# Two transformer blocks on one core: a ninth ring slot, held weight chunks spread, the last scatter ahead of modulation, and the last norm on token rows

## What is computed

```python
mod = silu(c) @ w_ada[i] + b_ada[i]            # 6 x 1024 for the tokens, as many for ctx
h = modulate(rmsnorm(x, g_norm1[i]), sh1, sc1)
ka, va, kb, vb, qa, qb, u, v, gates = _split(h @ w_in[i], KV_SIZES + Q_SIZES)
x = x + gt1 * branch_merge(ya, yb, yc, gates, w_branch[i], w_out[i])
h2 = modulate(rmsnorm(x, g_norm2[i]), sh2, sc2)
x = x + gt2 * ec_moe(h2, w_router[i], w_e1[i], w_e3[i], w_e2[i])
```

## Time and profile before

| | |
|---|---|
| median of 3 runs | 2883.66 us (2879.49 to 2886.35) |
| the profiled execution | 2883.96 us, its span 2882.2 us |
| TensorE busy | 2611.2 us, 91% |
| VectorE, ScalarE, GpSimd busy | 810.2, 449.5, 55.4 us |
| moved by the DMA engines | 663.81 MB, mean 230 GB/s |
| mean granted TensorE clock | 0.957 of full speed |

### The profile page before, as it was taken

How to read it: one execution, slowest core, us unless ns; L and a number is a source line. 1 busy time by engine, 2 the same in 40 slices (tenths; PEclk the granted TensorE clock), 3 DMA queues, 4 the chain that set the end, 5 groups by cost and what they waited for, 6 DMA issues and landing times.

```text
span 2882.2 us, 30967 instructions
## 1 busy us (share of the span) xinstructions
PE 2611.2 (91%) x13335; PEld 1547.2 (54%) x13335; DVE 810.2 (28%) x1764; ACT 449.5 (16%) x1002; POOL 55.4 (2%) x85
## 2 busy tenths in 40 slices
PE   8999999999999999999999898987999998666665
PEld 5678878578873445444444342332556885232322
DVE  2535511435512454332121121112344422010101
ACT  1320010230011022222021101112111311000001
POOL 1000000000003000000000000000200000000000
PEclk9999999999999999999999999999999999776877
DMA  8654444464456111121527999999721367999996
GB/s 276 222 162 149 173 161 146 163 217 146 169 173 168 67 59 59 44 73 59 204 105 324 420 421 421 421 421 386 178 88 67 124 262 322 421 421 421 420 421 259
DMA packets 201019, 663.81 MB, mean 230 GB/s; under 512 B 13426, under 2 KB 58784, under 8 KB 151732
## 3 DMA queue, kind: packets, MB, share of 16 engines
q1 hardware_dynamic: 192912, 641.97, 58.2%
q0 software_dynamic: 7776, 19.81, 3.1%
q10 hardware_dynamic: 196, 0.06, 0.0%
HBM read 660.67 MB, written 9.57 MB: 233 GB/s over the span
## 4 chain that ended last, share of the span: by engine, by line
PE 72%; DMA 23%; DVE 3%; ACT 2%; issue 1%; ACTq 0%; DVEq 0%
PE ps L506 40%; DMA ring<-in_w_e 22%; PE ps L527 8%; PE ps L1120 7%; PE ps L687 5%; PE ps L1074 1%; PE ps L622 1%; PE ps L1100 1%; PE ps L935 1%; PE ps L957 1%; PE ps L890 1%; PE ps L903 1%; DMA ring<-in_w_ada 1%; PE ps L878 1%; PE ps L553 1%
## 5 line engine op out<-in xcount | busy, mean ns | idle before, releaser
L506 PE MATMUL ps<-normed,ring 128*128 128x256 f32 (+1 forms) x3456 | 942.8, 433 | 12.4 <-ACT normed L2012 8.8
L506 PEld LDWEIGHTS ps<-normed,ring 128*128 128x128 f32 x3456 | 653.6, 191 | 279.3 <-issue 201.3
L1120 PE MATMUL ps<-ring,arena 128*32 128x256 f32 (+1 forms) x4384 | 595.4, 527 | 195.6 <-DMA ring<-in_w_e 187.3
L1120 PEld LDWEIGHTS ps<-ring,arena 128*32 128x32 f32 (+1 forms) x4384 | 194.9, 133 | 576.7 <-DMA ring<-in_w_e 286.8
L506 PE MATMUL ps<-arena,ring 128*128 128x256 f32 (+1 forms) x832 | 254.0, 462 | 1.3 <-DVE small L1248 1.3
L527 PE MATMUL ps<-ring,normed 128*128 128x512 f32 x512 | 222.8, 593 | 0.0
L506 PEld LDWEIGHTS ps<-arena,ring 128*128 128x128 f32 x832 | 156.1, 190 | 88.1 <-issue 73.1
L1329 DVE COPY arena<-ps 128x256 f32<-128x256 f32 (+1 forms) x102 | 55.9, 554 | 418.4 <-PE ps L506 173.1
L527 PEld LDWEIGHTS ps<-ring,normed 128*128 128x128 f32 x512 | 96.2, 190 | 116.2 <-issue 116.1
L687 PE MATMUL ps<-arena,ring 128*128 128x256 f32 x704 | 152.3, 379 | 0.0
L687 PEld LDWEIGHTS ps<-arena,ring 128*128 128x128 f32 x704 | 133.8, 190 | 18.2
(11 more groups left out here) (252 smaller groups left out, 1788.9 us busy)
## 6 DMA issues: line engine op xcount, KB each, us to landing
ring<-in_w_e SPq DMA_DIRECT2D x366, 1024.0 KB, 17.8
ring<-in_w_in SPq DMA_DIRECT2D x56, 1024.0 KB, 7.4
ring<-in_w_ada SPq DMA_DIRECT2D x48, 1024.0 KB, 7.4
ring<-in_ffn_w_up SPq DMA_DIRECT2D x88, 512.0 KB, 5.9
ring<-in_ffn_w_down SPq DMA_DIRECT2D x22, 1024.0 KB, 5.0
ring<-in_dil_w_qkv SPq DMA_DIRECT2D x18, 1024.0 KB, 5.1
arena<-in_w_e SPq DMA_DIRECT2D x14, 1024.0 KB, 13.2
ring<-in_sb_w_qkv SPq DMA_DIRECT2D x12, 1024.0 KB, 12.9
```

The lines of the kernel that those rows point to most:

```text
L506: ins = mm(o[:, 0:n], slots[k // 4][:, k % 4, f * P:(f + 1) * P], src[:, k, 0:n], start=k == 0, stop=k == kts - 1)
L1120: ins = mm(o[w * g:w * g + w, 0:cols], lhs(2 * c + j), slot[:, j, g * cols:(g + 1) * cols], start=c == 0 and j == 0, stop=c == KT // 2 - 1 ...
```

## The change

1. `NSLOT` = 9. Room for it comes from the constants (the tables of stick-breaking, 896 words, now go to the arena and are loaded when the rows staged there are used up; one unused table is dropped) and from a smaller scratch for DMA descriptors (4096 for 8192 bytes).
2. The chunks set aside are given by place, `ASIDE_AT`: in layer 0 numbers 8, 13, 18, 22, 27, 31, 36 and 40 of the experts' list, in layer 1 numbers 8 to 17.
3. Router: two parts (layer 0; one in layer 1) stand before the first transposes, one fold (none) and the last part behind them, and the last two folds behind the second transposes.
4. The two panels between the last expert of layer 0 and `scatter(3)` go: these two panels are now the ones used behind layer 1's sum of squares, with both folds before the first panel of `w_in`, and the last two panels follow that first panel.
5. The last norm: TensorE transposes X itself, ScalarE squares the token rows out of PSUM with a sum for each row, and VectorE multiplies the same PSUM rows by the row's factor and the gain (a row broadcast to all partitions, loaded at expert 12 of layer 1). The store is issued by token tiles, two times 512 KiB.
6. POOL: the dilated bias goes in three pieces each way, both layers' neighbourhood biases are written sheared during the first block, each to a tensor of its own, and the position tiles wait until VectorE has emptied the second panel of `w_in` (`tile_turn`).

```diff
-NSLOT = 8
+NSLOT = 9
+ASIDE_AT = ((8, 27, 22, 40, 18, 36, 13, 31), (8, 9, 10, 11, 12, 13, 14, 15, 16, 17))
...
         for c0 in (6, 7, 0, 1, 4, 2, 3, 5):
             panel(w, c0 * BRANCH)
+            if i and c0 == 6:
+                ada_panels(ADA_LAYER // 2)
...
-        held = [len(out) + NSLOT + j for j in range(ASIDE_FIRST[i] + ASIDE_THEN)]
+        held = [len(out) + at for at in ASIDE_AT[i]]
...
         if i == 0:
-            ada_panels(ADA_LAYER)
+            ada_panels(ADA_LAYER // 2)
...
             pe.wait_ge(loads["consts"], 16)
+            pe.wait_ge(loads["sb_tables"], 16)
...
                 if last:
                     ada_part()
                     ada_part()
+                    ada_fold()
+                    ada_fold()
                 gemm_T(1, H, qtok, fresh=True)
+                if last:
+                    ada_part()
+                    ada_part()
+                gemm_N(1, H, qtiles)
                 if last:
                     ada_fold()
                     ada_fold()
-                gemm_N(1, H, qtiles)
...
+                for _ in range(ADA_ROUTER[i] - 1):
+                    ada_part()
                 pe.wait_ge(aff_ready.sem, aff_ready.nth("pe"))
...
-                ada_gap(ADA_ROUTER[i])
+                for _ in range(ADA_ROUTER[i] - 2):
+                    ada_fold()
+                ada_part()
                 pe.wait_ge(pos_ready.sem, pos_ready.nth("pe"))
...
+                ada_fold()
+                ada_fold()
                 pe.wait_ge(P_ready.sem, P_ready.nth("pe"))
...
-                if not last:
-                    ada_part()
-                    ada_part()
                 scatter(3)
-                if not last:
-                    ada_fold()
-                    ada_fold()
...
-            mean_square(H, S)
-            for _ in range(KT // GRP):
-                pe.wait_ge(h_ready.sem, h_ready.nth("pe"))
-            for t in range(ST):
-                for half in range(2):
-                    o = banks.open("a")
-                    if banks.due:
-                        pe.wait_ge(*banks.due)
+            for half in range(2):
+                pe.wait_ge(banks.freed["v"], scattered[4 * half - KT + 3])
+                for t in range(ST):
+                    o = banks.open("a", "v")
+                    pe.wait_ge(*banks.due)
                     for f in range(4):
-                        ins = nc.tensor.transpose(o[:, f * P:(f + 1) * P], H[:, 4 * half + f, t * P:(t + 1) * P], ident)
+                        ins = nc.tensor.transpose(o[:, f * P:(f + 1) * P], X[:, 4 * half + f, t * P:(t + 1) * P], ident)
...
-            sp.wait_ge(final_ready.sem, final_ready.nth("sp"))
-            sp.dma_start(out[0].rearrange("(t p) d -> p t d", p=P), OUTT).then_inc(loads["out"], 16)
+            for t in range(ST):
+                sp.wait_ge(final_ready.sem, 2 * t + 2)
+                sp.dma_start(out[0, t * P:(t + 1) * P, :], OUTT[:, t, :]).then_inc(loads["out"], 16)
...
-            pre_norm(X, g_final)
+            v.wait_ge(ssq_ready.sem, ssq_ready.nth("v"))
+            ve.tensor_tensor(RCOL[:, 0:ST], SSQ[:, 0:ST, 0], SSQ[:, 0:ST, 1], ALU.add).then_inc(total_ready.sem, total_ready.up())
...
+            for t in range(ST):
+                for half in range(2):
+                    d = slice(half * 512, (half + 1) * 512)
+                    ve.scalar_tensor_tensor(OUTT[:, t, d], turned[t, half], RCOL[:, t:t + 1], FINAL_GAIN[:, d], ALU.mult, ALU.mult
+                                            ).then_inc(final_ready.sem, final_ready.up())
...
                 norm(X, 2 * S)
+                if last:
+                    ada_copies(ADA_LAYER // 2)
                 scale_shift(i, 0, 2)
...
-            norm(X, S)
+            table(LOG_EXP)
+            for half in range(2):
+                for t in range(ST):
...
+                    ins = se.activation(OUTT[:, t, half * 512:(half + 1) * 512], o, ACT.Square, accum_out=SSQ[:, t, half:half + 1])
...
+            for i in range(DEPTH):
+                gp.dma_start(rpb_scratch[:, :, 48:48 + 2 * NA_WIN_C - 1], a["na_rpb_2"][i]).then_inc(loads["rpb_out"], 16)
...
+                gp.wait_ge(tile_turn.sem, tile_turn.nth("gp"))
                 for hh in range(2):
...
+            gp.wait_ge(dma_free.sem, dma_free.nth("gp"))
+            gp.dma_start(FINAL_GAIN, dram(a["g_final_2"], 0, [[0, P], [1, D]])).then_inc(loads["final_gain"], 16)
...
-    nc = bacc.Bacc("TRN2", target_bir_lowering=False, num_devices=1, dynamic_dma_scratch_size=8192)
+    nc = bacc.Bacc("TRN2", target_bir_lowering=False, num_devices=1, dynamic_dma_scratch_size=4096)
```

96 lines of the change are left out of this document (58 added, 38 removed).

## The result

| | before | after |
|---|---|---|
| median of 4 runs | 2883.46 us (2879.49 to 2886.35) | 2859.36 us (2858.44 to 2859.77) |
| ratio of the runs | | 0.992, 95% interval 0.9908 to 0.9933 |
| the profiled execution, its span | 2883.96, 2882.2 us | 2858.44, 2856.6 us |
| mean granted TensorE clock | 0.957 | 0.954 |

What follows compares the result with a forecast made beforehand. DMA bytes bound both expert stages (2.49 us a chunk), TensorE or chains of engines the rest. Terms -3.2 + 0 - 5.0 - 5.6 - 2.2 + 1.2 - 6.9 = -21.7 us gave median 2862.0 us, range 2851 to 2872.

Steps and rivals of the forecast that it cites:

- Part 1, layer 0: Layer 0's router: modulation work moved around the transposes lets the gather start earlier, -3.2 us, bounds -4 and -1.5.
- Part 1, layer 1: Layer 1's router: the same move with two parts gains nothing, 0 us, bounds -1 and +2 for a slow start.
- Part 2: Ninth ring slot: one chunk more on board when each expert stage begins, -2.5 us each, -5.0 us together.
- Part 3: Layer 0's experts: spreading set-aside chunks closes an 8.5 us DMA hole and opens one of 2.9 us, net -5.6 us.
- Part 4: End of layer 0: scatter 7.35 us earlier, less parts and copies that come back in layer 1, net -2.2 us.
- The wait of lambda's exponential: Layer 1's first panel: the exponential comes some 16 us later, costs nothing, up to 3 us if free banks fail.
- Part 5: Small loads on POOL's queue stay hidden; only the final gain's load in layer 1's experts costs, +1.2 us.
- Part 6: Kernel's end: last norm on token rows, store by halves, shortens the tail by 6.9 us, bounds -8.5 and -5.
- rival C: Router's gather waits for something else and moved parts cost the scatter's gain: about -8 us, 2876 us, chance 0.05.
- A: Layer 0's spread gives its gain back: slots and spread bring 3 us in place of 10.6, 2869.6 us, chance 0.15.
- B: TensorE's clock falls to its lower level in layer 0's experts, making the kernel slower: 2931 us, chance 0.05.
- D: More gain: no new hole, full slots, harmless lambda wait, scatter -5, tail -8.5: about -31 us, 2852 us, chance 0.05.

Runs made afterwards that it cites:

- contig: The changed kernel with layer 0's eight set-aside chunks at numbers 8 to 15 again, nine slots kept; median 2866.78 us.
- slot8: The changed kernel with eight ring slots in place of nine, all else kept; median 2866.37 us.
- spread_late: The changed kernel with four of layer 0's eight set-aside chunks behind the first gather's expert (36, 40, 45, 50); median 2859.27 us.
- router_old: The changed kernel with all modulation parts and folds between the routers' first and second transposes again; median 2860.89 us.
- folds_late: The changed kernel with both routers' last two folds moved from ahead of the first gather to behind it; median 2858.46 us.
- combo2: The changed kernel with later set-aside chunks, router folds behind the gather, scaling before copies, both layer 1 router parts behind the first transposes; median 2854.21 us.
- ada_back: The changed kernel with two modulation parts between layer 0's last expert and last scatter again, one pair in layer 1; median 2863.00 us.
- before_tail: The kernel before with only the new last norm, its gain load and the store by halves; median 2872.60 us, ratio 0.9961.
- scale_first: The changed kernel with ScalarE scaling before its copies in layer 1's norm gap, first folds and second parts behind the first panel; median 2861.44 us.

## Why the prediction came out as it did, step by step

**What bounds the kernel.** That an expert stage ends after the chunks still to load x 2.49 us, and that only bytes on board, the start and holes count, was borne out three times: contig, slot8 and spread_late moved the end of layer 0's stage by 6.5, 3.6 and -2.3 us. The holes say 6.2 us for contig and -2.1 us for spread_late. For slot8 the count of one chunk says 2.5 us; the 3.6 us of bytes are the same stretch read once more at the same rate, not a second witness.

**Part 1, layer 0: forecast -3.2, measured -2.3 (router_old: 2.5).** The mechanism was right, the second transposes stand directly behind VectorE's product, 3.5 us closer to the router's start. The failed term is the one of the folds, "at most 0.5 us behind the selection". It was worked out by taking the old block's 9.7 us less three parts at full clock, 1.4 us a fold; in the trace before, the first two parts of that block took 5.05 us in place of 3.64 and the folds 1.0 us each. So the price for two, 2.8 us, was above their time at full clock and still too low: TensorE had been idle for 3.06 us and they took 3.62 us. The gather starts 3.8 us behind the second transposes, where it starts 2.4 us behind them in folds_late: the folds end 1.35 us behind the selection. The text had named a slow start as a bound and put it on the gather; it fell on the folds.

**Part 1, layer 1: forecast 0, measured +2.0, the end of its bounds.** The folds took 3.45 us and the gather 5.71 us, both for the most part at the lower level; 1.7 of the 2.0 us are the gather's. The sum counted how late the last fold ends, but took the price of the gather behind it from a trace in which parts had kept TensorE busy. combo2, which gives it that work back, has the gather at 4.04 us; router_old, which does so too, at 5.56 us. So the idle time made the gather slow in each trace that has it, and taking it away makes the gather fast in most, not in all.

**Part 2: forecast -2.5 in each stage; slot8 shows 3.6 and 2.7.** Right in layer 1. In layer 0 it is 1.1 us more, which no run explains and which is within what like traces differ by.

**Part 3: forecast -5.6; contig shows 6.5.** Old hole 8.6 us by windows (8.5 forecast), new hole 2.1 us (2.9 forecast), at the place forecast. The balance of 26 slots freed against 26 moved held to within 0.8 us. Both parts together: forecast -8.1, between the two traces -10.8, undone one by one 10.1. The 0.7 us that remain are within the difference between like traces.

**Part 4: forecast -2.2, measured -1.4 (ada_back: 1.5).** The stretch of the table has -2.7 us, but 1.4 us of it is the last down-projection, ahead of the edit (8.60 and 7.22 us for the same instructions). The scatter starts 7.37 us closer to the last matmuls (7.35 forecast). Of what comes back, the later scaling cost 1.4 us (1.5 forecast) and the two parts 3.6 us (3.64 forecast). The folds only changed places, as the sum had it. What the sum left out is TensorE's clock in the first panel of layer 1, 1.3 us: in after it is granted at 0.50 for most of 7 us there. At this place it falls in all eleven traces that have part 4, and stays at 1.00 in the three that don't (before, before_tail, ada_back). Which of the moves of part 4 lets it fall stays open. The wait of lambda's exponential cost TensorE nothing, as said: between the first panel's end and the next panel no idle time stands in the trace.

**Part 5: forecast +1.2, measured +1.3 (before_tail).** The early loads on GpSimd's queue cost nothing that shows: TensorE starts the first matmuls behind the stick-breaking tables at 76.42 us (76.60 before), and from 1985 to 2110 us the profile shows it waiting for no load. Up to layer 0's router the kernel is 0.5 us faster, less than the 0.8 us by which before and before_tail, alike up to there, differ.

**Part 6: forecast -6.9, measured -10.0, and -8.2 at the same clock.** The order of steps was right. Two terms were mis-sized. The transposes were priced at 3.65 us, the row behind 4.57 idle us; directly behind the scatter they take 1.91 us. And the scatter was taken at its 5.14 us; it took 3.72 us in this trace and 5.41 us in others. The halves' price held: 3.2 us forecast for the second half from the products' end to the end of the span, 3.0 measured; 4.4 for the whole, 4.4 measured. The Trainium skill, "DMA: Bandwidth & Descriptors", section Anatomy of one DMA, puts 2.0 us and bytes / 436 GB/s on a DMA, as a fit for those that GpSimd issues: by estimate 3.2 and 4.4 us for the two sizes. These stores are issued by SyncE, and both measurements come within 0.2 us of it.

**The sum** came within 2.4 us of the medians and 3.9 us of the spans, since the misses had both signs: -2.7 in parts 2 and 3, -3.1 in part 6, -0.5 upstream and -0.5 in part 4's stretch, where the 1.4 us of the down-projection were a gift of the clock and the 1.3 us of the first panel its price, against +0.9 and +2.0 in part 1. That these cancelled in part was luck. Two sums of the text are off by a microsecond or more and carry nothing: the bounds add up to -32 and -4, not -33 and -5, and what rival C leaves (slots -5.0, tail -6.9, gain +1.2) is -10.7 us, not about -8.

The rivals: A is out by contig. B, TensorE's clock in layer 0's experts, is out, as its clock is 1.00 from 1600 to 1936; but the clock that it took for a matter of the long stages decides over the short chains. C is out, as the gather came earlier (router_old) and part 4 won something (ada_back). D is out in after, which has the new hole; spread_late closes it.

## What to carry to other kernels

Where bytes bound a stage, count chunks: a hole in the DMA closes where a slot is freed in time, and its place and size come out of a balance of slots freed and chunks moved, to within a microsecond. When work is taken out from between two dependent steps, the engine that did it now idles there, and what follows may run at half the clock: price what TensorE does next from a row behind an equal idle time, not from its own row of before. Work moved out of a wait that covered it needs a new cover (the two folds in scale_first, 1.8 us); list what covered it. A low clock costs nothing while TensorE would wait for another engine's tiles anyway (the first panel in scale_first), and counts as soon as these are ready (the same panel in after).

## What the runs showed of the hardware

**The same instructions at two prices.** In the fourteen traces of this case the last 32 matmuls of layer 0's experts, always behind a wait of 2.43 us, took 7.1 to 7.2 us in six traces and 8.5 to 8.8 us in eight, and the last scatter 3.72 us in nine traces and 5.1 to 5.4 us in five. The two do not go together. No edit of this study explains which it is; spread_late lost its 2.3 us to it. With layer 1's gather (4.04 or 5.5 us) that is some 5 us, where the runs of the kernel before spread over 7 us (2879.49 to 2886.35). That the spread comes from there is argued, not shown, for each kernel was traced once. Its runs lean that way: among the nine on one chip the two fastest, 2878.13 and 2878.62 us, have a mean granted clock of 0.957 and 0.959, the two slowest, 2883.06 and 2883.80 us, 0.953 and 0.954. But a run of 2882.08 us on another chip has 0.959 too, and that mean holds layer 1's experts, whose length is the same within 0.3 us in all traces with nine slots. The Trainium skill, "TensorE: Matmul & The Clock Gate", section What's actually happening, says that the number of first matmuls at the lower clock varies from run to run of one kernel. No row here is of a kernel's first matmuls; the rows show the like in the middle of a kernel, from one kernel's trace to the next, behind waits of 1.3 to 2.5 us.

**Half a store.** The profile's DMA issues (KB each, median us from issue to landing) of after, and then of before:

```profile
out<-arena SPq DMA_DIRECT2D x2, 512.0 KB, 2.7
```

```profile
out<-arena SPq DMA_DIRECT2D x1, 1024.0 KB, 4.0
```

Half the bytes take two thirds of the time, and still the cut wins, since the first half goes while VectorE works on the second.
